# A product of zeros in each feed-forward of a two-block transformer kernel

## The reference

```
h = h + 0.5 * swiglu(rms_norm(h, ffn1_norm), ffn1_w_in, ffn1_w_out)      # 1024 -> 2 x 2816 -> 1024
...                                                                      # mixing
h = h + 0.5 * swiglu(rms_norm(h, ffn2_norm), ffn2_w_in, ffn2_w_out)
...
x = x + squared_relu_mlp(rms_norm_2(x, norm_mlp[layer]), mlp_w1[layer], mlp_w2[layer])   # 1024 -> 4096 -> 1024, layer 0 and 1
```

## Time and profile before

| | us |
|---|---|
| median of three runs | 1209.46 (1207.05 to 1209.95) |
| the profiled execution | 1206.77 |
| its span, first to last instruction | 1205.0 |
| TensorE (PE) busy | 1195.3 (99%) |
| weight loads (PEld) busy | 1059.0 (88%) |
| VectorE (DVE) busy | 859.4 (71%) |
| ScalarE (ACT) busy | 644.1 (53%) |
| GpSimd (POOL) busy | 226.7 (19%) |

### The profile page before, as it was taken

One profiled execution on the slowest core, in us unless ns is written; L12 is line 12 of the kernel. 1 busy time (PEld: TensorE's weight loads), 2 busy tenths in 40 slices (PEclk: granted clock), 3 DMA queues, 4 the chain that ended last, 5 costly groups with the idle time before them and its releaser, 6 DMA issues.

```text
span 1205.0 us, 19183 instructions
## 1 busy us (share of the span) xinstructions
PE 1195.3 (99%) x7641; PEld 1059.0 (88%) x7641; DVE 859.4 (71%) x1178; ACT 644.1 (53%) x860; POOL 226.7 (19%) x115
## 2 busy tenths in 40 slices
PE   9999999999999999999999999999999999999997
PEld 6888888988899888888999988888899978888886
DVE  6877667788868877766788786655679777766353
ACT  6655444465655755544643455544446784554442
POOL 1443301000000234310000024520000240445001
PEclk9999999999999999999999999999999999999999
DMA  8555545953345554555545555555576304555550
GB/s 316 210 175 189 195 176 175 298 191 107 105 149 180 178 202 176 181 198 180 175 149 200 178 207 190 194 178 191 191 257 233 140 19 175 184 200 176 178 206 35
DMA packets 31567, 218.03 MB, mean 181 GB/s; under 512 B 3584, under 2 KB 3856, under 8 KB 6272
## 3 DMA queue, kind: packets, MB, share of 16 engines
q1 hardware_dynamic: 29712, 210.06, 49.5%
q0 software_dynamic: 1488, 6.05, 1.7%
q10 hardware_dynamic: 288, 0.79, 0.2%
HBM read 215.82 MB, written 4.22 MB: 183 GB/s over the span
## 4 chain that ended last, share of the span: by engine, by line
PE 98%; DVE 1%; DMA 1%; ACT 0%; POOL 0%; issue 0%; SPq 0%; DVEq 0%; ACTq 0%; POOLq 0%
PE bank L1634 38%; PE bank L1635 19%; PE bank L1627 8%; PE bank L1628 8%; PE bank L1629 8%; PE bank L1812 2%; PE bank L1813 2%; PE bank L1814 2%; PE bank L2069 1%; PE bank L1743 1%; PE bank L1745 1%; PE bank L1744 1%; PE bank L1841 1%; DMA raw<-weights 1%; PE bank L1963 0%; PE bank L1946 0%
## 5 line engine op out<-in xcount | busy, mean ns | idle before, releaser
L858 DVE TENSOR_TENSOR w_hl<-raw,w_hl 128x2048 fp32r<-128x2048 f32 x194 | 444.1, 2289 | 135.0 <-ACT w_hl L438 134.1
L438 ACT ACTIVATE w_hl<-raw 128x2048 fp32r<-128x2048 f32 x195 | 370.5, 1903 | 138.0 <-PE bank L1635 49.5
L1634 PE MATMUL bank<-x_hl,w_hl 128*128 128x512 f32 x908 | 321.9, 399 | 0.0
L377 POOL TENSOR_TENSOR hidden<-hid_f,hidden 128x256 fp32r<-128x256 f32 (+1 forms) x76 | 189.3, 2491 | 527.6 <-ACT hidden L521 311.0
L1635 PE MATMUL bank<-x_hl,w_hl 128*128 128x256 f32 x908 | 255.0, 281 | 0.0
L1634 PE MATMUL bank<-hidden,w_hl 128*128 128x512 f32 x608 | 215.0, 399 | 0.0
L1634 PEld LDWEIGHTS bank<-x_hl,w_hl 128*128 128x128 f32 x908 | 170.6, 188 | 42.5 <-issue 0.2
L1635 PEld LDWEIGHTS bank<-x_hl,w_hl 128*128 128x128 f32 x908 | 171.5, 189 | 0.1
L1635 PE MATMUL bank<-hidden,w_hl 128*128 128x256 f32 x608 | 170.8, 281 | 0.0
L1634 PE MATMUL bank<-y_hl,w_hl 128*128 128x512 f32 x448 | 159.0, 400 | 0.0
L499 ACT ACTIVATE second<-bank 128x512 f32<-128x512 f32 (+1 forms) x100 | 54.4, 544 | 185.6 <-PE bank L1635 185.6
(11 more groups left out here) (389 smaller groups left out, 1706.0 us busy)
## 6 DMA issues: line engine op xcount, KB each, us to landing
raw<-weights SPq DMA_DIRECT2D x197, 1024.0 KB, 4.9
bias_skew<-bias_rows POOLq DMA_DIRECT2D x1, 3072.0 KB, 25.1
gate_or_bias<-bias_skew POOLq DMA_DIRECT2D x1, 2048.0 KB, 10.4
h<-x_t SPq DMA_DIRECT2D x2, 512.0 KB, 5.6
con<-consts SPq DMA_DIRECT2D x1, 769.5 KB, 12.6
raw<-weights ACTq DMA_DIRECT2D x1, 512.0 KB, 5.2
raw<-weights SPq DMA_DIRECT2D x1, 512.0 KB, 7.2
sv<-last_gain POOLq DMA_DIRECT2D x1, 512.0 KB, 3.7
```

The lines of the kernel that those rows point to most:

```text
L377: nc.gpsimd.tensor_tensor(hidden[:, at, 1, :], src, hidden[:, at, 0, :].bitcast(F32), ALU.subtract).then_inc(hid_lo, 1)
L438: nc.scalar.activation(dst, src, ACT.Copy).then_inc(hi_split, 1)
L858: V.tensor_tensor(w_lo[:, s, :], raw[:, s, :], w_hi[:, s, :].bitcast(F32), ALU.subtract).then_inc(lo_split, 1)
L1634: mm(out_, w_hi[:, s, c:c + m], x, start=start, stop=False, **kw)
```

## The change

`up` gets a new argument `idle`. Where it is set, one product of 64 columns is put in front of the fifth input tile (k = 4) of the first result tile (t = 0). Its weights are 128x128 of `zeros`, its moving operand 128x64 of `zeros`, and it adds to the first 64 columns of the bank that is being summed (`start=False`). It is set for chunk 2 in ffn1, and for chunk 1 in ffn2, mlp0 and mlp1: in each case the chunk right behind the norm's sum. So four products are added in the program, and nothing is removed.

```diff
+            def idle_product(out_):
+
+                mm(out_[:, 0:64], zeros[:, 0:P], zeros[:, 0:64], start=False, stop=False, skip_group_check=True)
+
-            def up(s, slot, x, pieces=None, first=False):
+            def up(s, slot, x, pieces=None, first=False, idle=False):
 
                 if pieces is None:
                     for t in range(2):
                         for k in range(KT):
+                            if idle and t == 0 and k == KT // 2:
+                                idle_product(bank[:, 2 * slot, :])
                             last = wide(bank[:, 2 * slot + t, :], s, k * 256 + t * P, P, x[:, k, :, :], k == 0,
                                         k == KT - 1)
...
-                        up((c0 + j) % RING, SLOTS[j % 3], x, stage if j == 0 else None, first).then_inc(chunk_used, 1)
+                        up((c0 + j) % RING, SLOTS[j % 3], x, stage if j == 0 else None, first,
+                           j == (2 if stage == "ffn1" else 1)).then_inc(chunk_used, 1)
```

## The result

The changed kernel takes 1196.17 us (median of four runs, 1195.86 to 1196.56), the kernel before 1208.56 us (median of four runs, 1207.05 to 1209.95: the three that are given above and one more). The ratio is 0.9898, 95% interval 0.9881 to 0.9915: 12.3 us less. A repetition of both gave 0.9915 (0.9898 to 0.9932). The forecast was 1198.4 us.

A forecast was written before the change was run, and what follows sets the result against it. TensorE, busy in 99% of the span, was taken as the bound. From the profiled 1206.77 us, less 11.5 for rhythm plus 0.44 price, came 1195.7; on the median's scale 1198.4 us, own range 1195.5 to 1201.5, 8-in-10 range 1195.5 to 1211.5.

The forecast's parts named there:

- What bounds the kernel: TensorE in the feed-forwards never idles; pairs start 0.3533 us apart, though products among their like make 0.3467 us.
- The price: Each zeros product in the four feed-forwards costs 0.11 us, 0.44 us in all (0.11 to 0.91), with no cover.
- The sign of 0.46 us: On PE's timeline, the pair before the zeros to the pair behind them: about 0.46 us instead of 0.35.
- The lower price by the issue floor: Products of up to 64 columns at about 25 ns in a stream: the four zeros products would cost 0.1 us.
- The rhythm: 1728 feed-forward pairs behind the zeros go at 0.3467 instead of 0.3533 us: 11.5 us gone.
- Rival 1: Behind the zeros the stream falls back to the three-pair pattern; only the price is left: 1209.9 us, chance 0.34.
- The reason given for the entry: At the zeros: a short product whose successor must wait for its load leads into the short rhythm; no separate size.
- the sentence that it hangs on a few nanoseconds: Such an entry is not sure to bring the short rhythm; a few nanoseconds decide, which rows can't work out.
- The time: Whole kernel: 1198.4 us on the scale of the median 1209.46 us, short rhythm in all four feed-forwards, chance 0.43.

The follow-up runs named there:

- the run with ffn1 alone: Changed kernel with the zeros product in ffn1 only, none in the other three feed-forwards: 1204.15 us, ratio 0.9972.
- the one with positions: Changed kernel with the zeros in front of k = 5, 6, 7 and 3 in ffn1, ffn2, mlp0 and mlp1: 1195.93 us.
- the one round the sum: Changed kernel, zeros moved: directly behind the norm's sum (ffn1), before chunk 2's first pair (mlp0), ahead of the sum (ffn2, mlp1): 1204.72 us.
- turned first chunks: Changed kernel, every second pair low weights first in each feed-forward's first chunk and the three output projections: 1195.90 us, ratio 0.9914.
- 56 columns: Changed kernel with zeros of 56, 60, 68 and 72 columns in ffn1, ffn2, mlp0 and mlp1: 1204.15 us.
- real 64 columns: Changed kernel without zeros; at k = 4 the 512-column product is done as 64 and then 448 columns, each with its load: 1207.46 us.

## Why the prediction was right

What bounds the kernel. Right: PE had no idle time to give, and the whole gain came out of the distance between starts. The estimate for that distance, from products among their like the earlier trace rows, was 0.3467 us, and the changed kernel has it: 1.04 us for three pairs.

The price. 0.11 us each was the choice; it is 0.133. Four of them make 0.53 us instead of 0.44. The reason given for it, that the next load can't start before the zeros' weights have moved on, is not what the rows show: that load starts 0.01 us behind the zeros' own (23.43, 23.42). Both start late, so the load behind the zeros has little to hide under. The sign of 0.46 us from the pair before the zeros to the pair behind them was off too: it is 0.40 (23.07 to 23.47), and the rest comes in the pair after (0.44, 23.47 to 23.91). The lower price by the issue floor that the Trainium skill gives (TensorE: Matmul & The Clock Gate, "Back-to-back issue gap") does not hold at this place. The same section of the Trainium skill says that its figure comes out too low for few columns, because it has no weight load in it, and the 0.133 us agree with that.

The rhythm. The term of 11.5 us was right stage by stage, to 0.02 us (the table above), once the price is 0.133. That a state is entered and then lasts was right: the run with ffn1 alone, the one with positions and the one round the sum show it. Rival 1, that the stream falls back, is refuted: same columns, same clock of 1.00, 454 pairs against 463.

The reason given for the entry was wrong. "Short, and the high weights behind it are not loaded when it is done" is as true of 16, 32 and 128 columns, and none of those did it. That the size in the change is the only one of the twelve tried from the slow rhythm that works was luck as far as this reason goes: by the same words 16 or 128 columns would have got the same forecast, and it would have been wrong. It was also too much to say that the norm's sum is no entry into the fast rhythm: in two traces of ffn1, and in all four stages with turned first chunks, the stream is out of the slow rhythm behind it. The forecast could have failed on the entry; the trace of before held one such piece that was fast and one that was not the earlier trace rows, and the sentence that it hangs on a few nanoseconds that can't be worked out was the better one. What the entry needs is not settled: 64 columns of bf16 behind a pair have it, at all three phases of the slow pattern, and 60 and 68 have not.

The time. 1198.4 was forecast, 1196.17 measured. The sum against the profiled execution was 1195.7 for one that took 1206.77 us before, and the changed kernel's profiled execution took 1196.12. The 2.7 us that I put on top, for the distance between that execution and the median, did not come back: the spread of before (1207.05 to 1209.95) is not that of after (1195.86 to 1196.56).

Why before spreads more is shown only in part. Over 38 executions beside the experiments it took 1203.27 to 1209.81 us. The seven from 1209.29 us on have a mean granted clock of 0.996 or 0.997, and the six up to 1204.16 us one of 0.998 or 0.999: the high end goes with the clock (the last section has where it falls). The six lowest lie some 3.3 us below the middle, as much as one feed-forward in the fast rhythm gives. That ffn1's sum now and then leads out of the slow rhythm by itself was seen in two traces (56 columns, real 64 columns), but no execution of before near 1203.5 was profiled, so that this is their reason stays open.

## What to carry to other kernels

Where an engine is busy without a gap, subtract starts: if the same instructions stand further apart in one stretch than the sum of what their kinds take elsewhere in the trace, the difference may be a pattern that the stream has locked into, and it can be taken back without removing work. Alternating products of 512 and 256 columns with their own loads lost 2% here. A fix by one added product is brittle (its size, its type and what stands ahead all matter, and one float32 product behind it undoes it), so it belongs where a trace shows that it took; turning every second pair asks for none of that and brought three quarters of the gain on each pair.

## What the runs showed of the hardware that was not expected

The rhythm itself: the same 512- and 256-column products at the same granted clock of 1.00 settle at 1.06 or at 1.04 us for three pairs, and stay there for hundreds of pairs over waits of new chunks. In ffn1, which of the two follows the norm's sum went with the place in the three-pair pattern at which the sum came (0.35 us ahead of it: slow, nine traces; 0.36 us: not slow, two traces).

And the granted clock in the sparse attention. In some executions it falls to the lower level for a while, in others not, with the same instructions. Windows of all engines (PE, PEld, DVE, ACT, POOL, then the clock), ffn1 alone:

```profile
940.00:950.00 10.00, 10.00 (x81) 9.21 (x80) 7.87 (x13) 6.54 (x21) 4.87 (x2) 0.93 0.54 193
950.00:960.00 10.00, 10.00 (x77) 9.45 (x77) 7.43 (x44) 7.44 (x29) 2.90 (x2) 0.90 0.05 20
```

PE is busy in all of both stretches, as it is before them. 0.93 and 0.90 are a part of the stretch at 1.2 GHz and the rest at 2.4. It fell there in 7 of the 14 profiled executions of all kernels here. With that the stage took 138.36 us (883.48 to 1021.84 by its sums) against the 137.2 of the kernels before and after, where the clock is 1.00 throughout. With zeros in every chunk it was 0.71 in 950 to 960, and the stage took 141.05 us (884.27 to 1025.32). That is why such small changes are better read from a stage's own starts than from one total time.
